# Half of a projection's contraction by Strassen's block products, with gated values kept in memory: a hybrid attention layer on one core

## The reference

```python
z = jnp.einsum('bld,dc->blc', h, w_in)           # one projection, 6672 columns
fq, fk, fv, fg, ff, sq, sk, sv, sg = jnp.split(z, idx, axis=-1)
lf = jax.nn.log_sigmoid((ff + b_f).astype(jnp.float32))
...
fo = fox_prompt(fq, fk, fv, lf) * jax.nn.silu(fg)
so = swa_prompt(sq, sk, sv, sinks, rel_bias) * jax.nn.silu(sg)
out = jnp.einsum('blc,cd->bld', jnp.concatenate([fo, so], axis=-1), w_out)
hp = layer_norm(ALPHA * hp + out_p, ln_g[l], ln_b[l])
```

## Time and profile before

| | |
|---|---|
| Median of 3 runs | 1066.47 us (1066.45 to 1066.72) |
| The profiled execution's own time | 1065.04 us |
| Its span, first to last instruction | 1063.5 us |
| Mean granted TensorE clock | 0.997 |
| PE busy | 1048.2 us, 99% |
| DVE / ACT busy | 565.5 (53%) / 421.6 us (40%) |
| Matmuls | 7587 |
| Bytes moved | 106.64 MB, mean 100 GB/s |

### The profile page before, as it was taken

One profiled execution on the slowest core, in us unless ns is written; L12 is line 12 of the kernel. 1 busy time (PEld: TensorE's weight loads), 2 busy tenths in 40 slices (PEclk: granted clock), 3 DMA queues, 4 the chain that ended last, 5 costly groups with the idle time before them and its releaser, 6 DMA issues.

```text
span 1063.5 us, 19599 instructions
## 1 busy us (share of the span) xinstructions
PE 1048.2 (99%) x7587; PEld 981.1 (92%) x7587; DVE 565.5 (53%) x1206; ACT 421.6 (40%) x968; POOL 51.4 (5%) x103
## 2 busy tenths in 40 slices
PE   8999999999999999999999999999999999999996
PEld 7999999999999999999999999999999878888884
DVE  6655464544636455364544565544665574332586
ACT  6434343434435344353434454334544552111300
POOL 2010000000000000000000000000000000000000
PEclk9999999999999999999999999999999999999998
DMA  9143123132222223123522212122121154222423
GB/s 337 56 138 108 57 102 112 51 120 93 72 90 102 81 81 120 66 77 112 196 75 93 88 47 79 47 101 94 61 73 61 66 198 140 79 79 100 176 61 118
DMA packets 20808, 106.64 MB, mean 100 GB/s; under 512 B 3216, under 2 KB 3632, under 8 KB 11488
## 3 DMA queue, kind: packets, MB, share of 16 engines
q1 hardware_dynamic: 14960, 83.13, 22.1%
q0 software_dynamic: 5808, 22.95, 6.5%
HBM read 95.18 MB, written 14.17 MB: 103 GB/s over the span
## 4 chain that ended last, share of the span: by engine, by line
PE 97%; DVE 1%; DMA 1%; ACT 0%; SPq 0%; issue 0%; DVEq 0%; ACTq 0%
PE ps L1186 63%; PE ps L1340 19%; PE ps L1310 5%; PE ps L1286 4%; PE ps L1269 2%; PE ps L1270 2%; PE ps L1219 1%; PE ps L1325 1%; DMA x_raw<-in_xT 1%; PE ps L1289 0%; DVE rows L1155 0%; DVE rows L1165 0%; ACT k L685 0%; SPq L498 0%; DVE xl L980 0%
## 5 line engine op out<-in xcount | busy, mean ns | idle before, releaser
L1186 PE MATMUL ps<-xh,wh 128*128 128x288 f32 (+1 forms) x1664 | 504.7, 303 | 0.4 <-DVE wl L988 0.4
L1186 PE MATMUL ps<-xl,wh 128*128 128x288 f32 (+1 forms) x1664 | 492.7, 296 | 0.0
L1186 PE MATMUL ps<-xh,wl 128*128 128x288 f32 (+1 forms) x1664 | 492.4, 296 | 0.0
L1186 PEld LDWEIGHTS ps<-xh,wh 128*128 128x128 f32 x1664 | 313.0, 188 | 6.6 <-issue 4.1
L1186 PEld LDWEIGHTS ps<-xl,wh 128*128 128x128 f32 x1664 | 313.5, 188 | 0.0
L1186 PEld LDWEIGHTS ps<-xh,wl 128*128 128x128 f32 x1664 | 312.8, 188 | 0.0
L825 DVE TENSOR_TENSOR wl<-w_raw,wh 128x1024 fp32r<-128x1024 f32 x132 | 160.2, 1221 | 98.8 <-ACT wh L650 97.7
L1340 PE MATMUL ps<-wh,mix_parts 128*128 128x512 f32 x576 | 185.4, 391 | 0.0
L650 ACT ACTIVATE wh<-w_raw 128x1024 fp32r<-128x1024 f32 x132 | 137.9, 1053 | 77.1 <-PE ps L1340 70.0
L702 ACT ACTIVATE tb<-tb,small 128x256 f32<-128x256 f32 (+5 forms) x160 | 81.3, 509 | 145.8 <-DVE small L915 101.4
L1340 PEld LDWEIGHTS ps<-wh,mix_parts 128*128 128x128 f32 x576 | 108.1, 188 | 23.3 <-issue 1.0
(11 more groups left out here) (126 smaller groups left out, 791.8 us busy)
## 6 DMA issues: line engine op xcount, KB each, us to landing
w_raw<-in_w_all SPq DMA_DIRECT2D x66, 1024.0 KB, 4.8
cbc<-c_rows POOLq DMA_DIRECT2D x16, 360.0 KB, 4.1
x_raw<-in_xT SPq DMA_DIRECT2D x7, 592.0 KB, 10.3
rows<-in_x_p POOLq DMA_DIRECT2D x4, 1024.0 KB, 5.5
out_y_p<-rows SPq DMA_DIRECT2D x16, 256.0 KB, 2.5
rel_copies<-rel_rows POOLq DMA_DIRECT2D x1, 3072.0 KB, 13.6
out_fvT<-vT POOLq DMA_DIRECT2D x8, 296.0 KB, 3.5
out_fkT<-kT POOLq DMA_DIRECT2D x8, 296.0 KB, 2.8
```

What stands on the lines that cost most here:

```text
L1186: ins = nc.tensor.matmul(ps[:, st.bank(k, h), 0:width], a[k % 2][:, w], b[:, ko, first:first + width], start=(ko == 0 and i == 0), stop=(k ...
```

## The change

The tiles are taken in duos (v with g, q with k, g with q): 26 of them. The first is projected as before, the other 25 in 15 units of 12 matmuls. The first 8 of 16 chunks are seen as a 2x2 block product: the two tiles by two groups of four chunks (A and B) on the side of the weights, two groups of chunks by two token halves (early, late; 296 columns each) on the side of x. It is computed by the Winograd form of Strassen's algorithm with seven block products of 4 chunks x 3 matmuls instead of eight: units 0, 1, 2, 3, 6, 7 and 10. The other 8 chunks stay plain (units 4, 5, 8, 9, 11 to 14); where an output block has one product of its own left, it is accumulated in the same bank as its plain part. A third bank (SIDE, 7) is used beside TOP (0) and BOTTOM (1).

DVE makes four sums of weight parts per duo (128x512: seven, five, six, four), each of which is split into high and low parts like a weight, and after the products it adds their results: `take_six`, `take_seven`, `take_five`, and `join` for each of the four output blocks. What the block products need of x (four differences, and their high and low parts) is made once, in the opening. Weights are loaded in halves of a tile, four transfers a duo.

SBUF is laid out anew. mixT holds two pairs; the gated values of the first 14 pairs are stored to memory (`store_mixed`, POOL) and read back near the end in five transfers (SP) into the space of the x sums and beside it. The steps of the attention are set anew, the Stretch of pair 1 is no longer in the loop, and the zero fills of POOL and the loads of the residual rows come later.

The diff, cut to its core:

```diff
-STEPS = 8
+UNITS = 15
+DUOS = PROJ_TILES // 2
+CUT = KO // 4
+CUT_LEN = CUT * P
+HALF = TOK // 2
...
+            run(Stretch(["qk"], 1, own=Fox, pair=0, kv=0, first=True))
+            run(Stretch(["vg", "qk"], 2, own=Fox, pair=1, kv=1, kind=Fox, g=0, kvs=1))
+            with engine.Fori(2, FOX_PAIRS) as g:
+                run(Stretch(["vg", "qk"], 2 * g, own=Fox, pair=g, kv=g, kind=Fox, g=g - 1, kvs=g))
...
+                    run(Stretch(["gq"], g + (d0 + 1 - first), own=Swa, pair=g, kind=Swa, g=g - 1,
                                 kvs=FOX_PAIRS + m + 1, turn_before=g - 2, keep=True))
...
+            score = [2, 4, 6, 8, 9]
+        turn = [x + 4 for x in score] if final or len(duos) == 2 else [6, 8, 9, 12, 13]
...
+                sp.wait_ge(*((four_made, d) if f == 0 else (right_low, d)))
+                load_part(d + 1, f, FRONT, front_loaded)
+            def load_next_back(d):
+                sp.wait_ge(back_low[1], d)
+                load_part(d + 1, 1, BACK, back_loaded)
+            with sp.Fori(1, DUOS - 1) as d:
+                load_next_front(d, 1)
+                load_next_front(d, 0)
+                load_next_back(d)
+                sp.wait_ge(back_low[0], d + 1)
+                load_part(d + 2, 0, BACK, back_loaded)
...
+                pool.wait_ge(gated, 2 * g + 2)
+                pool.sem_inc(pool_passed, 1)
+                src = mixT[:, bass.ds(g & 1, 1), :].rearrange("p a n -> p (a n)")
+                pool.dma_start(mix_rows[bass.ds(g, 1)].rearrange("a p n -> p (a n)"), src).then_inc(mix_stored, 16)
...
+            def keep_first(st, k):
+                act.wait_ge(unit_done, st.after(k, 0))
+                if st.first:
+                    act.wait_ge(silu_done, 2)
+                else:
+                    act.wait_ge(bottom_summed, st.duo(k) - 1)
+                nc.scalar.activation(first_part[:], ps[:, TOP, 0:HALF], ACT.Copy).then_inc(first_kept, 1)
...
+                for i, (high, raw) in enumerate(((sum7_high, raw7), (sum6_high, raw6), (sum3_high, raw3))):
+                    act.wait_ge(sum_made, i + 1)
+                    nc.scalar.activation(high[:], raw[:], ACT.Copy).then_inc(sum_high, 1)
+                front_parts(1, (passed, 1))
                 gates()
+                seven_part(1, (passed, 2))
+                six_part(1, (passed, 2))
+                for h, done in enumerate((v_read, v_first)):
+                    act.wait_ge(projected[h], 1)
+                    if h == 0:
+                        keep_meta(ps[:, 0, 0:N_META])
+                    nc.scalar.activation(vT[:, h * HALF:(h + 1) * HALF], ps[:, h, 0:HALF], ACT.Copy).then_inc(done, 1)
...
+                        if u == 1:
+                            five_part(d, (unit_done, st.after(k, 0)))
+                        if u == 2:
+                            right_part(d, (unit_done, st.after(k, 1)))
+                        if u == FIRST_SUM_AT and st.first:
+                            sum_five()
+                        if u == 4:
+                            four_part(d)
+                            back_parts(d, 1, (projected[1], 2) if st.first else (unit_done, st.after(k, -1)))
+                        if u == 8 and not last:
+                            front_parts(d + 1, (unit_done, st.after(k, 6)))
+                        if u == 11 and not last:
+                            seven_part(d + 1, (unit_done, st.after(k, 10)))
+                            six_part(d + 1, (unit_done, st.after(k, 7)))
+                        if u == 13 and not last:
+                            back_parts(d + 1, 0, (unit_done, st.after(k, 12)))
...
+                nc.vector.tensor_tensor(w_sum[:, A], w_raw[1][:, A], w_raw[1][:, B], ALU.add).then_inc(seven_made, 1)
...
+                nc.vector.tensor_tensor(w_raw[1][:, A], w_raw[1][:, A], w_raw[0][:, A], ALU.add).then_inc(five_made, 1)
...
+                nc.vector.tensor_tensor(w_raw[0][:, A], w_raw[0][:, A], w_sum[:, A], ALU.add).then_inc(six_made, 1)
...
+                nc.vector.tensor_tensor(w_sum[:, B], w_raw[0][:, A], w_raw[0][:, B], ALU.add).then_inc(four_made, 1)
...
+                nc.vector.tensor_tensor(diff_part[:], ps[:, SIDE, 0:HALF], first_part[:], ALU.subtract).then_inc(diff_made, 1)
...
+                nc.vector.tensor_tensor(mid_part[:], ps[:, BOTTOM, 0:HALF], diff_part[:], ALU.add).then_inc(mid_made, 1)
...
+                five = ps[:, BOTTOM, 0:HALF]
+                nc.vector.tensor_tensor(diff_part[:], five, diff_part[:], ALU.add).then_inc(over_made, 1)
+                nc.vector.tensor_tensor(last_part[:], five, mid_part[:], ALU.add).then_inc(under_made, 1)
...
+                    (0, 0): (TOP, first_kept, 5, ALU.add, corner_summed),
+                    (1, 0): (SIDE, over_made, 9, ALU.add, side_summed),
+                    (0, 1): (TOP, mid_made, 12, ALU.subtract, top_summed),
+                    (1, 1): (BOTTOM, under_made, 14, ALU.add, bottom_summed)}[f, h]
+                dve.wait_ge(unit_done, st.after(k, last))
+                dve.wait_ge(part_ready, d)
...
+                nc.vector.tensor_tensor(out, ps[:, bank, a], part[:, a], op).then_inc(summed, 1)
...
+                nc.vector.tensor_tensor(raw7[:], x21, x11, ALU.subtract).then_inc(sum_made, 1)
+                dve.wait_ge(sum_made, 1)
+                nc.vector.tensor_tensor(raw6[:], x22, raw7[:], ALU.subtract).then_inc(sum_made, 1)
+                dve.wait_ge(sum_made, 2)
+                nc.vector.tensor_tensor(raw3[:], x12, raw6[:], ALU.subtract).then_inc(sum_made, 1)
+                nc.vector.tensor_tensor(x21, x21, x22, ALU.subtract).then_inc(sum_made, 1)
+                dve.wait_ge(sum_made, 3)
+                for i, (low, raw, high) in enumerate(((sum7_low, raw7, sum7_high), (sum6_low, raw6, sum6_high),
+                                                      (sum3_low, raw3, sum3_high))):
+                    dve.wait_ge(sum_high, i + 1)
+                    low_of(low[:], raw[:], high[:], sum_low)
+                front_parts(1)
+                dve.wait_ge(own_made, 3)
+                gate_logs()
+                make_seven(1, (passed, 2))
+                make_five(1)
+                make_six(1)
+                seven_part(1)
+                six_part(1)
                 dve.wait_ge(small_loaded, 4 * 16)
                 bias_table()
+                back_parts(1, 0)
...
+                    if u == 0 and 1 <= k <= len(st.duos):
+                        join(st, k - 1, 1, 1)
+                        ready = (k - 1, 1, 1)
+                    if inside:
+                        if u == 2:
+                            take_six(st, k)
+                        if u == 3:
+                            take_seven(st, k)
+                        if u == 6:
+                            join(st, k, 0, 0)
+                            ready = (k, 0, 0)
+                        if u == 7:
+                            take_five(st, k)
+                        if u == 10:
+                            join(st, k, 1, 0)
+                            ready = (k, 1, 0)
+                        if u == 13:
+                            join(st, k, 0, 1)
+                            ready = (k, 0, 1)
...
+                        if u == 1:
+                            five_part(d)
+                        if u == 2:
+                            right_part(d)
+                        if u == FIRST_SUM_AT + 1 and st.first:
+                            sum_five()
+                        if u == 3:
+                            make_four(d, (unit_done, st.after(k, 2)))
+                        if u == 4:
+                            four_part(d)
+                        if u == 5:
+                            back_parts(d, 1)
+                        if not last:
+                            if u == 8:
+                                front_parts(d + 1)
+                            if u == 9:
+                                make_seven(d + 1, (unit_done, st.after(k, 7)))
+                                make_five(d + 1)
+                            if u == 10:
+                                make_six(d + 1)
+                            if u == 11:
+                                seven_part(d + 1)
+                            if u == 12:
+                                six_part(d + 1)
+                            if u == 14:
+                                back_parts(d + 1, 0)
...
+                        ins = nc.tensor.matmul(ps[:, bank, 0:HALF], a[:, w], b[:, j, :], start=(start and j == 0 and i == 0),
+                                               stop=(stop and j == CUT - 1 and i == 2))
...
+                if u == 0:
+                    if st.first:
+                        pe.wait_ge(v_read, 1)
+                    else:
+                        pe.wait_ge(top_summed, d - 1)
+                    pe.wait_ge(front_low, d)
+                    ins = block_product(TOP, of_tile(0, A), of_x(first_x, early), True, True)
+                elif u == 1:
```

(56 more changed lines are left out.)

684 lines of the change are left out of this document (445 added, 239 removed).

## The result

| | before | after |
|---|---|---|
| Median of the runs | 1066.46 us | 1090.61 us (1089.44 to 1091.57, 4 runs) |
| Ratio to before | | 1.0229 (1.0211 to 1.0247) |
| Profiled execution / its span | 1065.04 / 1063.5 us | 1090.5 / 1089.0 us |
| Mean granted clock | 0.997 | 0.987 |

The account below looks back on a forecast made before the run. PE was taken as the bound, busy 1048.2 of 1063.5 us. 1065.04 - 36.2 (matmuls) + 8.0 (opening) + 7.2 (window pairs) + 6.4 (forgetting stretches) = 1050.4; the run median lies 1.4 higher, so 1052 us, range 1037 to 1065.

Parts of the forecast that it names:

- Matmuls removed: In 25 duos, 180 matmuls replace 192 each; 1.48 us saved in 19 duos, 1.34 in 6, together 36.2 us.
- DVE's extra work: Per duo +8.6 us on DVE, loading it 82% in forgetting pairs and 88% in two-tile window pairs; about 215 us busier.
- Window pair: Two-tile window pairs: PE waits for the turned fourth block, 0.7 to 1.9 us, taken as 1.2; 7.2 us for six.
- the window pairs last over 35 us: Sign that the prediction is wrong; two-tile window pairs were forecast near 33.6 us.
- Forgetting stretch, first half: First turned block comes late for PE by 0.4 to 1.0 us, taken as 0.8; 6.4 us for eight stretches.
- Forgetting stretch, second half: Second duo has no attention in its later half, so its cover was called ample; no stall counted.
- Opening: PE waits 4.5 us for ACT's v copies, then about 1.2 (gate transposes), 2.1 (unit 6), 0.3 (unit 8); together 8 us.
- The clock: Rival, chance 0.08: the opening's 4.5 us wait drops the clock; units at half clock cost 1.6 to 3.3 us, giving 1054 to 1055.
- Loads: Four half loads per duo, each half of a transfer landing in 4.8 us, stay hidden; DMA engines 27% used at most.
- The slower rival: Chance 0.10: DVE's queue becomes the bound in window pairs and forgetting stretches' first duos; 14 stalls of 2.6 us give 1074.7.
- The central case at 0.50: The forecast itself, 1052 us for the whole kernel, kept at chance 0.50.
- the high bounds of all stalls: Opening 12 us, window pairs 3 each, forgetting stretches 2 each, all at their upper ends: 1076 us.

Follow-up runs that it names:

- the version with three moves: Changed kernel with turned copies ahead of the tanh, cached keys split at step 20, first turned block copied ahead of the v or k copies: 1043.67 us.
- the first move: Changed kernel with ACT copying turned blocks ahead of the tanh and weight copies in stretches of one duo: 1067.12 us, 1.0016 of before.
- the version with both moves: Changed kernel with turned copies ahead of the tanh and the cached keys' split at step 20: 1051.05 us, 0.9867 of before.

## Why the prediction was wrong

Against the profiled execution the sum said 1050.4 and the trace has 1090.5: 40.1 too low. Of that, 27.6 is PE idle time (49.2 measured, 8.0 + 7.2 + 6.4 = 21.6 forecast) and 12.5 PE busy time, 10.2 of it the clock, which the sum left out. Of the 27.6 us of idle time, 10.9 are the window pairs and 13.8 the keys; 2.8 more are the sixth row of the waits above, which no term of the sum had.

- **Matmuls removed, 36.2 us: right.** 7287 matmuls, and where no wait disturbs, stages of 60.29 and 32.30 us against 60.3 and 32.4.
- **DVE's extra work: right**, +199.7 us for about 215. So was the reading that 82 to 88% of load is not yet a bound: the version with three moves has the same load and no such wait.
- **Window pair: this step failed.** The walk of the queues was right: counted from 660.67, where the block products start, the top join ended after 28.8 (28.2 to 29.3 forecast) and the turned copy after 30.7 (30.1 to 31.3). Wrong was what it was held against: "PE wants it after 14 units and the attention before them ... 29.4". That is where the values want the block. The transpose of the fifth block, one unit earlier, wants it too, since it writes into the bank that the copy empties, and PE was there at 688.27, after 27.6. The stall is 3.2 instead of 1.2, in six stretches, the last 2.0: 18.1 us for 7.2. The range's upper end for it, 3 us each, was about right, and the sign "the window pairs last over 35 us" came true at 35.56.
- **Forgetting stretch, first half: right.** 0.8 us each forecast, 6.7 us in 8 waits measured.
- **Forgetting stretch, second half: this step failed too.** The sentence "The second duo has no attention in its later half, so its cover is ample" took the q, k duo as free without a walk. It ends in the longest chain of the stretch: cached keys, weight sum six, two low parts, top join, q copies, back weight parts, last join, four k copies, low parts, scores. The scores waited 1.03 + 0.46 us after each of nine such duos: 13.8 us in 19 waits, forecast at nothing, and moving the cached keys out of the chain gave 15.5.
- **Opening: the first wait right, the total in part luck.** v was copied at 48.40 (48.4 forecast), and PE was idle for 4.7 us (4.5). Of the three later waits, forecast as 1.2 + 2.1 + 0.3, only that of unit 6 came, with 0.7; the 1.7 us for the top join of the first duo was not in the list. The total, 7.2 against 8.0, comes near because one wait that nobody forecast stands in for three that fell short.
- **The clock: left out of the sum, and a rival at 0.08 that happened beside the others.** In after's windows right behind the 3.2 us waits the granted clock was 0.69, 0.54 and 0.54 in three cases and 1.00 in two; the first of each:

```profile
618.90:622.00 3.10, 3.10 (x18) 2.81 (x20) 0.66 (x1) 0.60 (x1) 0.00 (x0) 0.69 0.37 111
655.90:659.00 3.10, 3.10 (x33) 2.86 (x33) 0.71 (x1) 0.60 (x1) 0.00 (x0) 1.00 0.32 110
...
49.00:56.00 7.00, 7.00 (x37) 7.00 (x38) 5.94 (x38) 5.45 (x9) 0.68 (x2) 0.68 0.25 78
53.35:84.92 31.57, 28.98 (x201) 28.06 (x199) 23.36 (x43) 14.14 (x26) 6.21 (x13) 0.94 0.38 115
```

  The third row is the opening, behind the 4.7 us wait. The last holds the 3.4 us at 0.50 from 80.8, and the only wait shortly before them is the one of 1.7 us that ended at 79.49. So the length of one wait did not decide it here. The mistake was to make the clock a case of its own: every case with such waits can bring it along. The Trainium skill (TensorE: Matmul & The Clock Gate, HAM oscillation) says that long idle gaps bring the throttle back; here that holds behind three of five gaps of 3.2 us, not behind the other two, and the clock also fell behind one of 1.7 us.
- **Loads: "hidden" held for this kernel, but only behind other waits.** The sum priced each half load by a transfer that lands in 4.8 us and took 27% of the DMA engines' time as the most. In the stretch of the 3 MB copy the share is 0.55 in after (it was already 0.51 from 500 to 535 us of before), and the load issued there took 10.8 us in the version with three moves. In after ACT already waited 2.0 us for the weights of the copy's stretch, which cost PE nothing; with the queues in order it cost 1.4.
- **The slower rival** had its place half right (window pairs, 14 stretches at 2.6 us) and named load as the mechanism. The runs show order: 46.9 us, from 1090.6 to 1043.7, came from moving three operations, with no work taken away. Taking away the sums, 50 of the 200 us of added DVE work, gave 8.9 more, 3.6 of them in the stretch of the copy; the other 150 us were never taken away.

The chances were too sure. The central case at 0.50 rested on two walks of the queue, although the point that one of them was held against had been read off only one of its readers, and a third place was not walked. Even the high bounds of all stalls, 1076, lie below 1090.6, since the keys and the clock stood in the sum at nothing.

## What to carry to other kernels

When work is added to an in-order queue, list for each result every reader with its step, also the one that only waits for the space (the next transpose into the same bank), and take the earliest. Walk the stretches without much work as well: the last link of a long chain decides, not the load. If such a change comes out slower, look for what PE waits longest for and move that one small operation ahead of those that wait, before giving the change up: 2.3% slower became 2.2% faster here.

## What the runs showed of the hardware that was not expected

- Removing a PE wait can give more than the wait: the first move took away 18.1 us of waits and 23.5 us of time, with 4.4 us less PE busy time, most of it clock.
- A half clock ahead of a wait can be free. In the version with both moves the clock was 0.84 from 15 to 25 us, and 1.00 in after, yet the opening took no longer (52.19 against 53.35 us to the same instruction). PE came to the wait for vT 1.3 us later (45.40 against 44.13) and still had to wait, 2.3 instead of 4.7 us. The other 1.15 us of the shorter wait are not the clock's: ACT's copy to vT was that much earlier in this run (47.25 against 48.40). The windows, first of that version, then of after:

```profile
15.00:25.00 10.00, 10.00 (x66) 9.81 (x65) 9.03 (x7) 8.34 (x8) 0.00 (x0) 0.84 1.02 413
```

```profile
15.00:25.00 10.00, 10.00 (x76) 9.80 (x76) 7.88 (x8) 7.89 (x7) 0.00 (x0) 1.00 1.02 417
```

- A 3 MB copy at the side stretched a 512 KB load of weights, usually about 4 us, to 10.8 us, so that ACT stood for 3.63 us; with the copy in two parts the load took 5.9 us. One transfer in GpSimd's queue can make one of SyncE's late.
